# Cutting three expert gathers of a transformer kernel into transfers of 120 and 8 rows, each followed by a nine-row copy

## What is computed

```python
def chunk(xc):                                   # 128 tokens
    q = (xc @ w_query).reshape(128, 8, 2, half)
    s = jnp.einsum('thpk,pnk->thpn', q, sub_keys)
    sv, si = lax.top_k(s, 16)
    cand = sums of the 16 x 16 pairs; cidx = si0 * 128 + si1
    top_s, sel = lax.top_k(cand, 16)
    eidx = jnp.take_along_axis(cidx, sel, axis=-1)   # 16 experts per head and token
    g = jax.nn.softmax(top_s, axis=-1)
    u, vv = expert_down[eidx], expert_up[eidx]
    act = gelu(einsum('td,thkd->thk', xc, u))
    return einsum('thk,thkd->td', g * act, vv)
```

## Time and profile before

| what | value |
|---|---|
| median of 3 runs | 2239.84 us (2239.53 to 2241.55) |
| profiled execution, its own time | 2241.91 us |
| span of that execution, first to last instruction | 2240.1 us |
| PE / DVE / ACT / POOL busy | 1990.3 / 1609.4 / 1144.5 / 874.5 us |
| moved by DMA | 707.23 MB, of it 536.90 MB by the gathers |
| gathers of layer 0 / layer 1 | about 735 to 1386 us / 1583 to 2232 us |

### The profile page before, as it was taken

One profiled execution on the slowest core, in us unless ns is written; L12 is line 12 of the kernel. 1 busy time (PEld: TensorE's weight loads), 2 busy tenths in 40 slices (PEclk: granted clock), 3 DMA queues, 4 the chain that ended last, 5 costly groups with the idle time before them and its releaser, 6 DMA issues.

```text
span 2240.1 us, 29611 instructions
## 1 busy us (share of the span) xinstructions
PE 1990.3 (89%) x9760; PEld 1302.1 (58%) x9798; DVE 1609.4 (72%) x3230; ACT 1144.5 (51%) x2534; POOL 874.5 (39%) x557
## 2 busy tenths in 40 slices
PE   9999999999999898977777788999899887778877
PEld 8999899998889644422222223889644432222222
DVE  4566777777787877776777765787887776777774
ACT  4455555545554655454454545565655444444443
POOL 0120000000230355566667663040355566666664
PEclk9999999999999999999999999999999999999999
DMA  7544465665636999999999997736899999999998
GB/s 247 172 132 142 148 184 180 185 189 157 219 119 219 381 421 421 421 421 421 421 418 422 420 421 302 233 116 222 334 421 421 421 421 421 422 422 411 422 421 338
DMA packets 120772, 707.23 MB, mean 316 GB/s; under 512 B 13664, under 2 KB 13920, under 8 KB 55008
## 3 DMA queue, kind: packets, MB, share of 16 engines
q0 software_dynamic: 73728, 536.90, 57.8%
q1 hardware_dynamic: 43488, 157.63, 22.4%
q10 hardware_dynamic: 3456, 11.40, 1.5%
HBM read 704.84 MB, written 1.05 MB: 315 GB/s over the span
## 4 chain that ended last, share of the span: by engine, by line
PE 41%; DMA 25%; POOL 11%; DVE 9%; issue 8%; ACT 6%; POOLq 0%; SPq 0%; DVEq 0%; ACTq 0%
DMA work<-in_experts,expert_idx 24%; PE ps L548 11%; POOL work L1098 10%; PE ps L549 10%; PE ps L550 10%; PE ps L1315 6%; DVE work L2166 2%; DVE weights_lo L533 2%; PE ps L687 1%; ACT L1616 1%; ACT L1667 1%; DMA weights<-in_wstream 1%; ACT arena L1672 1%; DVE work L2143 1%; PE ps L713 1%
## 5 line engine op out<-in xcount | busy, mean ns | idle before, releaser
L1315 PE MATMUL ps<-work,arena 128*128 128x512 f32 x2040 | 989.9, 617 | 216.1 <-ACT arena L1672 212.4
L1098 POOL DMA_INDIRECT work<-in_experts,expert_idx x512 | 790.2, 1543 | 621.2 <-PE ps L1315 291.3
L1315 PEld LDWEIGHTS ps<-work,arena 128*128 128x128 f32 x2040 | 359.0, 191 | 821.0 <-ACT arena L1672 516.2
L2166 DVE CUSTOM_DVE_ANT_0 work<-h_norm,work 128x1024 f32<-128x1024 f32 x480 | 588.1, 1225 | 334.5 <-DMA work<-in_experts,expert_idx 320.2
L1667 ACT ACTIVATE small<-small 128x1 f32<-128x1 f32 x512 | 150.2, 293 | 609.1 <-DVE small L2166 588.0
L533 DVE TENSOR_TENSOR weights_lo<-weights,weights_hi 128x1024 fp32r<-128x1024 f32 x280 | 349.8, 1255 | 152.8 <-ACT weights_hi L528 152.1
L548 PE MATMUL ps<-feat_hi,weights_hi 128*128 128x256 f32 x1528 | 445.3, 291 | 7.6 <-DVE weights_lo L533 5.8
L528 ACT ACTIVATE weights_hi<-weights 128x1024 fp32r<-128x1024 f32 x280 | 295.0, 1056 | 286.0 <-PE ps L550 232.6
L549 PE MATMUL ps<-feat_lo,weights_hi 128*128 128x256 f32 x1528 | 432.8, 283 | 0.0
L550 PE MATMUL ps<-feat_hi,weights_lo 128*128 128x256 f32 x1528 | 432.7, 283 | 0.0
L548 PEld LDWEIGHTS ps<-feat_hi,weights_hi 128*128 128x128 f32 x1528 | 293.3, 192 | 18.1 <-issue 9.3
(11 more groups left out here) (250 smaller groups left out, 1912.1 us busy)
## 6 DMA issues: line engine op xcount, KB each, us to landing
weights<-in_wstream SPq DMA_DIRECT2D x280, 512.0 KB, 4.2
work<-in_experts,expert_idx POOLq DMA_INDIRECT x512
arena<-in_wstream SPq DMA_DIRECT2D x12, 512.0 KB, 6.0
arena<-in_na_bias ACTq DMA_DIRECT2D x6, 512.0 KB, 5.3
params<-in_wstream SPq DMA_DIRECT2D x6, 512.0 KB, 5.9
arena<-in_bias ACTq DMA_DIRECT2D x5, 512.0 KB, 4.6
params<-in_par ACTq DMA_DIRECT2D x2, 576.0 KB, 5.3
params<-in_par ACTq DMA_DIRECT2D x1, 1024.0 KB, 6.7
```

What stands on the lines that cost most here:

```text
L1098: nc.gpsimd.indirect_dma_start(ring[:, r, :], None, experts, bass.IndirectOffsetOnAxis(ap=EIDX[:, b, c * RING + r:c * RING + r + 1], axis= ...
L1315: ins = nc.tensor.matmul(bank(2 * t + h), DIAG[:, r, :], ring[:, r, D + h * 512:D + (h + 1) * 512], start=False, stop=False)
L2166: nc.vector.tensor_tensor_reduce(ring[:, r, 0:D], HN[:, t, :], ring[:, r, 0:D], 1.0, 0.0, ALU.mult, ALU.add, hd[:, r:r + 1]).then_inc(dots ...
```

## The change

In the second pass of the second step of each layer, the gathers of slots 1, 3 and 5 (numbers 25, 27 and 29) are cut. POOL issues an indirect DMA for rows 0 to 119, waits for `rest_index`, issues a second one for rows 120 to 127, whose indices it takes from a small tile `REST`, and then a plain copy of nine rows of 8 numbers from the constants in HBM to unused columns of `SMALL` (`move_share`). The second part has a semaphore of its own, and DVE waits for both before the dot. `REST` starts at partition 0 and is filled by a copy that SP issues (`rest_moved`) once `routed` says that the second step's indices are there; in SP's queue it stands ahead of the first weight half of the next layer, and for layer 1 ahead of the output. At the end SP also waits for the six small copies. The class `Turns` only gives up five unused semaphores.

```diff
+SHARED = (1, 3, 5)
+SHARED_ROWS = 120
+MOVED = 9
+MOVES = 3
...
+        REST = sb("rest_idx", [P - SHARED_ROWS, RING], U32)
...
+            def rest_moved(l):
+
+                sp.wait_ge(routed, l * ROUTES + 2)
+                sp.dma_start(REST[:, :], EIDX[SHARED_ROWS:P, 1, RING:2 * RING]).then_inc(rest_index, 16)
+
             for n in range(SLOTS + whole * SLOTS, HALVES):
                 l, local = divmod(n - L_HALF, L_HALVES)
+                if local == 0 and l:
+                    rest_moved(l - 1)
...
+            rest_moved(LAYERS - 1)
+            sp.wait_ge(share_moved, 16 * LAYERS * MOVES)
...
+                def gather_part(rows, index, r, landed):
+
+                    nc.gpsimd.indirect_dma_start(ring[rows, r, :], None, experts,
+                                                 bass.IndirectOffsetOnAxis(ap=index, axis=0)).then_inc(landed, 16)
+
+                def move_share(n, nth):
+
+                    at = 400 + 8 * (l * MOVES + nth)
+                    nc.gpsimd.dma_start(SMALL[0:n, at:at + 8], consts[0:n, 0:8]).then_inc(share_moved, 16)
+
+                def gather_shared(b, c, r, use):
+
+                    wait_alone(pool, slot_used[r], use + 1, pool_passed)
+                    gather_part(slice(0, SHARED_ROWS), EIDX[0:SHARED_ROWS, b, c * RING + r:c * RING + r + 1], r, g_landed[r])
+                    wait_alone(pool, rest_index, 16 * l + 16, pool_passed)
+                    gather_part(slice(SHARED_ROWS, P), REST[:, r:r + 1], r, rest_landed[SHARED.index(r)])
+                    move_share(MOVED, SHARED.index(r))
...
-                            gather(b, c, r, l * USES + k * PASSES + c)
+                            if c and r in shared:
+                                gather_shared(b, c, r, l * USES + k * PASSES + c)
+                            else:
+                                gather(b, c, r, l * USES + k * PASSES + c)
...
-                gathers(1, 1)
+                gathers(1, 1, SHARED)
...
                             dve.wait_ge(g_landed[r], use * 16 + 16)
+                            if shared and c and r in SHARED:
+                                dve.wait_ge(rest_landed[SHARED.index(r)], 16 * l + 16)
```

More of the change, by code:

```diff
@@ L299, in build @@
         g_landed = [sem(f"g_landed{i}") for i in range(RING)]
+        rest_landed = [sem(f"rest_landed{r}") for r in SHARED]
+        rest_index, share_moved = sem("rest_index"), sem("share_moved")
         slot_used = [sem(f"slot_used{i}") for i in range(RING)]
@@ L308, in build, with __init__ @@
         pool_passed, dve_passed = sem("pool_waits_passed"), sem("dve_waits_passed")
-        class Norm:
+        class Turns:
             def __init__(self, name):
+                self.xp = sem(name + "_transposed")
+                self.hi = sem(name + "_hi")
+                self.hT = sem(name + "_hT")
+        class Norm(Turns):
+            def __init__(self, name):
+                super().__init__(name)
                 self.sq = sem(name + "_squares")
@@ L318, in __init__ @@
                 self.hn = sem(name + "_normed")
-                self.xp = sem(name + "_transposed")
-                self.hi = sem(name + "_hi")
-                self.hT = sem(name + "_hT")
         n_attn, n_post, n_ffn = Norm("n_attn"), Norm("n_post"), Norm("n_ffn")
-        n_mix, n_peer = Norm("n_mix"), Norm("n_peer")
+        n_mix, n_peer = Turns("n_mix"), Norm("n_peer")
         def root_table(col):
@@ L1100, in gather, with gathers @@
                         bass.IndirectOffsetOnAxis(ap=EIDX[:, b, c * RING + r:c * RING + r + 1], axis=0)).then_inc(g_landed[r], 16)
-                def gathers(k, b):
+                def gather_part(rows, index, r, landed):
[10 more added lines that the diff above has]
+                    move_share(MOVED, SHARED.index(r))
+                def gathers(k, b, shared=()):
                     wait_alone(pool, routed, l * ROUTES + k + 1, pool_passed)
@@ L2152, in _, with step_dve @@
                 rc.restart()
-                def step_dve(t, k, b, uses, mixed=None, ahead=2):
+                def step_dve(t, k, b, uses, mixed=None, ahead=2, shared=False):
                     rc = Chain(dve, route_step)
@@ L2199, in mixed @@
                             lo_query(2 * (PQ_FIRST + k) + 1 + r // 2)
-                    step_dve(0, k, k % 2, l * USES + k * PASSES, mixed)
+                    step_dve(0, k, k % 2, l * USES + k * PASSES, mixed, shared=k == 1)
                 with dve.Fori(0, PH // 2 - 1) as i:
```

## The result

The changed kernel takes **2266.38 us** (median of 4 runs, 2264.53 to 2268.76) against 2239.78 (2239.53 to 2241.55) for the kernel before beside it: ratio 1.0118, 95% interval 1.01 to 1.0135. It is 26.6 us slower, where 5.8 us faster was forecast, and far outside the range given.

What follows compares the result with a forecast made beforehand. All 16 DMA engines bound the PEER gathers, one ending last; 6.5 us relief per layer, less idle time and small losses, leaves 3.2 and 2.6: 2241.91 - 5.8 = 2236.1 us, as a median 2234.0; 8-in-10 range 2231.5 to 2241.5.

Steps and rivals of the forecast that it cites:

- the price of the cut gathers on the DMA engines: In the cut gathers, each 8 KB row takes 0.311 us; 21 rows fewer relieve one engine of 6.5 us per layer.
- What bounds the kernel: In both PEER layers' gathers all 16 DMA engines are always busy at 421 GB/s; one engine ends last, by 3.7 and 3.5 us.
- One engine gets no share of 120 rows: In each cut gather, 15 engines take 8 rows each; the one left out has 1 row or none in place of 8.
- It is the slow engine: The engine left out of the cut gathers is the one that ends each layer; all the gain depends on it.
- the gain of 5.8 us: Time won at the ends of the two layers' gathers after idle time: 3.2 and 2.6 us.
- rival 3: Another engine than the slowest is relieved, or a different one each time: 2239.8 to 2241.7 us, or 2237.6; chance 0.20.
- six new DMAs at 1.84 us each: POOL's added DMAs ahead of gather 30 in each layer cost 11.0 us, bounds 7.4 to 14.0.
- The delay at gather 30: POOL issues gather 30 of each layer 6.1 us late, bounds 2.5 to 9.1, after making up 4.9 us of waiting.
- The index copy, POOL's wait for it, the moved weight half, SP's waits: Edits on SP and POOL around the cut gathers: all hidden, zero cost; the index tile is ready 11 us early.
- Rival 4: POOL becomes the bound for a while because its new DMAs are dear, such as 4 us copies: 2248.3 us; chance 0.08.
- The signs to look for: Profile after: short tails, dots 3 us earlier; gather 30 near 812 us; third, DMA share dips one engine for 3 us, 800-830.
- The first of the signs of being wrong: At the layers' ends, tail windows still showing one engine alone for 3 us would make the forecast wrong.

Runs made afterwards that it cites:

- e12: Kernel before plus series of eight equal transfers behind its work, from SP, then POOL; from SP partitions 0-63 ran at 203 GB/s, 32-95 at 421.
- e3: Changed kernel with only the 120-row transfers; rows 120 to 127 of the three gathers per layer and the copies left out: 2267.68 us.
- e14: Kernel before plus series of POOL gathers round the eight slots: whole 64.6 us; with three 0-63 68.3, three 32-95 61.2, three cut into 120 and 8 78.5.
- e9: Changed kernel with the three gathers per layer fetching only 64 rows into partitions 32 to 95, no other rows, no copies: 2232.55 us.
- e11: Changed kernel with 60 rows into partitions 32 to 91 in the three gathers, the rest left out, copies of 9 and 8 rows: 2233.9 us.
- e2: Changed kernel with whole gathers again, keeping the nine-row copies, SP's index copy and POOL's wait: 2241.34 us.
- e1: Changed kernel with whole gathers and no nine-row copies, keeping SP's index copy and POOL's wait for it: 2240.25 us.

## Why the prediction was wrong

**The step that failed is the price of the cut gathers on the DMA engines**: "A row of 8 KB at 26.3 GB/s takes 0.311 us". That rate came from rows in which every gather wrote all 128 partitions, and it was carried over to transfers that write 120 and 8. Measured, such a row took 0.61 us in a series of 120-row transfers (e12), the rows of the stretch 800:820 of e3 took 0.59, and whole gathers beside the cut ones were slowed with them (e14). All that the change might cost was looked for on POOL and in waits; that a row could take longer once it is cut off was no term of the sum and no rival. It is the largest term: 4.4 us for each of six gathers, +26.6 us.

Point by point:

- *What bounds the kernel*: right. In these stretches the time follows the bytes that the engines move: what the windows lack, 27.9 us, is the loss, and e9 wins 8.8 us for 7.5 us of bytes less. This is also why nothing covered the half rate.
- *One engine gets no share of 120 rows*: right for SP's queue, by the share of 0.95 in e12. For POOL's, which the kernel uses, no view shows it.
- *It is the slow engine*: not borne out, and so the gain of 5.8 us is missing from the sum as well. The changed kernel and e11 both end with one engine alone for 3.1 to 4.1 us. That is the premise of rival 3, but its time did not come out.
- *POOL*: six new DMAs at 1.84 us each were too dear. With its gap an 8-row gather takes 1.2 us and a copy 0.89 at most, below the lower bound of 1.23. The delay at gather 30 was 1.5 us and not 6.1, below its lower bound of 2.5 too. In e2 the copies cost nothing that can be measured.
- *The index copy, POOL's wait for it, the moved weight half, SP's waits*: nothing that can be measured, as said (e1).
- *Rival 4, slower because POOL becomes the bound*: the sign came true and the mechanism didn't. It put the danger in the issuing engine, and the danger was in the transfer.
- *The signs to look for*: the third was the right place, "between 800 and 830 us", and the wrong column. The share did not dip, the rate did. The first of the signs of being wrong came true: one engine is alone at the end for 3 us and more.

No row of the kernel before shows a transfer of 8 KB rows to part of the partitions, so none could have named 208 GB/s. But POOL's new DMAs weren't in the trace either and got bounds and a rival; the rate of the cut gathers got neither. A rival in which cut gathers run at half rate would have had the sign of the result.

## What to carry to other kernels

A transfer to fewer than 128 partitions isn't a part of a whole one: cut by rows it can fall from 421 to about 205 GB/s and slow its neighbours, so where DMA is the bound and rows are long, leave whole transfers whole, and if half a tile is enough, write partitions 32 to 95 and not 0 to 63. Read share and rate together: here a share of 1.0 with half the rate meant rows that took twice as long each, not engines short of work. And before relieving an engine, find out which one is behind.

## What the runs showed of the hardware that was not expected

- The rates by partitions written, with rows of 8 KB, from SP (e12): 0-127 424, 32-95 421, 0-111 271, 0-95 246, 0-119 208, 0-63 203, 64-127 202 GB/s. More partitions are not always faster.
- With three cuts near each other, cutting a gather into 120 and 8 rows costs 4.4 to 4.6 us each, more than the 2.49 us of a whole gather, as whole gathers beside it take up to 4.84 us.
- POOL issues a plain nine-row copy in 0.57 to 0.59 us and an 8-row indirect one in 0.88 to 0.89, less than any whole gather (0.93 at least).
- TensorE's granted clock fell with the starved stretch: in e3 it was 1.00 in 780:800, where PE ran 71 matmuls in 20 us, 0.90 in 800:810 with 15 in 10 us, and 0.50 (1.2 GHz) in 810:820 with 9. It did not set the time: in 830:840 of e3 the gathers ran at 421 GB/s again at a granted clock of 0.83.
